# One overflow loop nested by four, one ring slot kept for the next stage's weights, and routing constants loaded once, in a fused two-block transformer kernel

## What is computed

```python
def _hier_moe(t, wr_g, br_g, wr_e, br_e, w_gate, w_up, w_down):
    lg = (t @ wr_g) + br_g                      # 4 groups
    g = argmax(lg); gate_g = softmax(lg)[g]
    le_g = ((t @ wr_e) + br_e).reshape(n_tok, 4, 8)[g]
    top_v, top_i = lax.top_k(le_g, 2)           # 2 of 8 experts in the group
    weights = gate_g * softmax(top_v)
    ...
    hidden = silu(x_blk @ w_gate[e]) * (x_blk @ w_up[e])     # 1024 -> 512
    y = hidden @ w_down[e]                                   # 512 -> 1024
    out[token] += y * weight
```

## Time and profile before

| what | value |
|---|---|
| time, median of 3 runs | 3021.82 us (3021.67 to 3022.43) |
| the profiled execution's own time | 3016.29 us |
| its span in the profile | 3014.4 us |
| PE busy | 2466.3 us, 82% |
| VectorE busy | 999.0 us, 33% |
| ScalarE busy | 560.1 us, 19% |
| GpSimd busy | 175.7 us, 6% |
| data moved by DMA | 591.83 MB, mean 196 GB/s |

### The profile page before, as it was taken

The page is one execution under the profiler, slowest core; times in us unless marked ns, Lnnn a source line. Parts: engine busy times, 40 slices in busy tenths (PEclk is TensorE's granted clock), DMA queues, the critical chain, the costliest instruction groups (busy, mean ns, idle before and its releaser), DMA issues. The chain is left out here.

```text
span 3014.4 us, 30863 instructions
## 1 busy us (share of the span) xinstructions
PE 2466.3 (82%) x11973; PEld 1302.9 (43%) x11973; DVE 999.0 (33%) x2199; ACT 560.1 (19%) x1254; POOL 175.7 (6%) x278
## 2 busy tenths in 40 slices
PE   7999898876977777598985977776696778999999
PEld 2443366444533333245643634333243544444444
DVE  3211276644222222466544222221365343001000
ACT  2000177210000000116510000000123441000000
POOL 0000000001211111000001211111001000000000
PEclk9999999887999999798987999999797789999999
DMA  7554100517999998410238999996500120321210
GB/s 299 179 185 166 60 1 1 212 74 307 415 415 416 416 415 326 178 42 19 72 130 347 414 416 415 415 415 283 211 14 3 46 70 24 143 84 56 84 56 28
DMA packets 143249, 591.83 MB, mean 196 GB/s; under 512 B 21460, under 2 KB 24028, under 8 KB 104192
## 3 DMA queue, kind: packets, MB, share of 16 engines
q1 hardware_dynamic: 132544, 568.83, 48.0%
q0 software_dynamic: 10560, 21.01, 1.9%
HBM read 579.19 MB, written 24.22 MB: 200 GB/s over the span
## 5 line engine op out<-in xcount | busy, mean ns | idle before, releaser
L1776 PE MATMUL moe_down<-moe_wd,moe_hid_t 128*64 128x512 f32 x1024 | 244.0, 620 | 73.2 <-DMA moe_wd<-in_moe_w_down 61.2
L1750 PE MATMUL moe_up<-moe_wu,moe_xg_t 128*64 128x256 f32 x2048 | 236.4, 383 | 62.3 <-DMA moe_wu<-in_moe_w_up 62.1
L1750 PE MATMUL moe_gate<-moe_wg,moe_xg_t 128*64 128x256 f32 x2048 | 240.0, 388 | 53.8 <-DMA moe_wg<-in_moe_w_gate 52.2
L395 PE MATMUL qkv_acc<-qkv_w,a_buffer 128*128 128x512 f32 x576 | 256.2, 598 | 1.4 <-DVE a_buffer L470 1.2
L2637 PE MATMUL mlp_acc<-m_h,mlp_w 128*128 128x512 f32 x512 | 223.1, 596 | 10.9 <-DMA mlp_w<-in_w_up 8.9
L1750 PEld LDWEIGHTS moe_gate<-moe_wg,moe_xg_t 128*64 128x64 f32 x2048 | 154.3, 139 | 161.4 <-DMA moe_wg<-in_moe_w_gate 89.7
L2652 PE MATMUL mlp_acc<-mlp_w,mlp_u_t 128*128 128x512 f32 x512 | 220.0, 592 | 1.4 <-DVE mlp_u_t L2672 1.4
L1750 PEld LDWEIGHTS moe_up<-moe_wu,moe_xg_t 128*64 128x64 f32 x2048 | 151.5, 137 | 143.7 <-DMA moe_wu<-in_moe_w_up 83.2
L395 PEld LDWEIGHTS qkv_acc<-qkv_w,a_buffer 128*128 128x128 f32 x576 | 107.4, 191 | 132.7 <-issue 123.9
L1776 PEld LDWEIGHTS moe_down<-moe_wd,moe_hid_t 128*64 128x64 f32 x1024 | 74.2, 141 | 201.8 <-issue 129.7
L1836 DVE COPY moe_y<-moe_down 128x512 f32<-128x512 f32 x64 | 44.2, 691 | 351.6 <-PE moe_down L1776 351.6
(11 more groups left out here) (360 smaller groups left out, 2838.4 us busy)
## 6 DMA issues: line engine op xcount, KB each, us to landing
moe_wg<-in_moe_w_gate SPq DMA_DIRECT2D x64, 2048.0 KB, 30.5
moe_wu<-in_moe_w_up SPq DMA_DIRECT2D x64, 2048.0 KB, 29.5
moe_wd<-in_moe_w_down SPq DMA_DIRECT2D x64, 2048.0 KB, 30.4
qkv_mod_w<-in_mod_w SPq DMA_DIRECT2D x48, 1024.0 KB, 4.9
mlp_w<-in_w_up SPq DMA_DIRECT2D x8, 2048.0 KB, 9.2
mlp_w<-in_w_down SPq DMA_DIRECT2D x8, 2048.0 KB, 7.8
qkv_w<-in_a_w_qkv SPq DMA_DIRECT2D x12, 1024.0 KB, 9.3
in_w<-in_w_in SPq DMA_DIRECT2D x4, 2048.0 KB, 19.0
```

The costliest lines, as they stand in the source:

```text
L395: mm = nc.tensor.matmul(acc[i % 4][:], h_t[:, k, t * P:(t + 1) * P], w[:, c % w_ring, k, :], start=(k == 0), stop=(k == KD - 1))
L1750: mm = nc.tensor.matmul(acc[b][halves[f], 0:HF], xg_t[b][:, k, c, :], w[:, c, k, f * HF:(f + 1) * HF], start=(c, k) == (0, 0), stop=(c, k) ...
L1776: mm = nc.tensor.matmul(down[b][halves[c], :], hid_t[:, k, h, :], wd[z][:, 2 * h + k, c * NCHUNK:(c + 1) * NCHUNK], start=(k, h) == (0, 0) ...
```

## The change

Three things change.

1. `before`, `iota`, `rowid` and `half` become buffers that live through the program. They are loaded in `qkv0`, right behind `ones`; the four loads and the two waits for them leave `route0` and `route1`.
2. Slot 0 of the ring holds expert 0 and no other expert of that layer. Experts 1 to 31 alternate between slots 1 and 2, so expert i waits for expert i - 2. Behind its last refill SP waits for `downed` >= 1 and loads 3 x 2 MB of the next stage's weights into slot 0: all of `b_w_qkv` in layer 0, three of the five chunks of `w_in_2` in layer 1. `qkv1` and `in2` read these chunks from there; `in2` loads the other two itself.
3. The overflow loops become `while_left`: `nx // 4` turns (6 and 4), the four bodies nested in each other's condition, so that a turn without overflow makes one test.

```diff
-            sp.dma_start(e["ones"][:], e["c_ones"]).then_inc(s["ones_in"], 16)
+            for name in ("ones", "before", "iota", "rowid", "half"):
+                sp.dma_start(e[name], e[f"c_{name}"]).then_inc(s["ones_in"], 16)
...
-            loads = [
-                (before[:], e["c_before"]), (iota[:], e["c_iota"]), (rowid[:], e["c_rowid"]),
-                (half[:], e["c_half"]),
-            ]
-            for dst, src in loads:
-                sp.dma_start(dst, src).then_inc(s["const_in"], 16)
...
-            pe.wait_ge(s["const_in"], 16 * 4)
...
-            dve.wait_ge(s["const_in"], 16 * 4)
...
+def slot_and_fill(i):
+
+    return (0, 1) if i == 0 else (1 + (i + 1) % 2, (i + 1) // 2)
+
+
+def next_chunks(ring):
+
+    flat = [ring["wg"][0][:].rearrange("p c k n -> p (c k n)"),
+            ring["wu"][0][:].rearrange("p c k n -> p (c k n)"),
+            ring["wd"][0][:].rearrange("p k n -> p (k n)")]
+    return [x.rearrange("p (k n) -> p k n", k=KD) for x in flat]
...
+def while_left(eng, nx, n, one):
+
+    with eng.Fori(0, nx // 4) as i4:
+        with eng.If(4 * i4 < n):
+            one(i4, 0)
+            with eng.If(4 * i4 + 1 < n):
+                one(i4, 1)
+                with eng.If(4 * i4 + 2 < n):
+                    one(i4, 2)
+                    with eng.If(4 * i4 + 3 < n):
+                        one(i4, 3)
...
             for i in range(RING, NE):
-                refill(i - RING + 1, i % RING, i)
+                refill(i - 1, slot_and_fill(i)[0], i)
+            sp.wait_ge(s["downed"], 1)
+            view = next_w.rearrange("(k p) n -> p k n", p=P)
+            for c, dst in enumerate(next_chunks(ring)):
+                sp.dma_start(dst, view[:, :, c * NCHUNK:(c + 1) * NCHUNK]).then_inc(
+                    ring["next_in"][c], 16)
...
-            with pool.Fori(0, nx // 2) as i2:
-                for b in range(2):
-                    i = NE + 2 * i2 + b
-                    with pool.If(2 * i2 + b < n):
-                        pool.wait_ge(s["turned_x"], i + 1)
...
+            def one_extra(i4, j):
+                i, b = NE + 4 * i4 + j, j % 2
+                pool.wait_ge(s["turned_x"], i + 1)
...
+            while_left(pool, nx, n, one_extra)
...
-        w = ph.sb("w", [P, 3, KD, NCHUNK])
+        w = next_chunks(ring)
...
-            for c in range(3):
-                sp.dma_start(w[:, c], view[:, :, c * NCHUNK:(c + 1) * NCHUNK]).then_inc(loaded[c], 16)
...
             for c, (n0, width) in enumerate(chunks):
-                sp.dma_start(w[:, :, n0:n0 + width], view[:, :, n0:n0 + width]).then_inc(loaded[c], 16)
+                if c >= 3:
+                    sp.dma_start(w[c], view[:, :, n0:n0 + width]).then_inc(loaded[c], 16)
```

More of the change, by code:

```diff
@@ L1391, in route @@
     with Phase(nc, f"route{layer}") as ph:
[L1392 to L1395, removed]
+        before, iota, rowid, half = (e[x] for x in ("before", "iota", "rowid", "half"))
         gate_t = ph.sb("gate_t", [P, nt, NG])
@@ L1611, in load_down, with experts @@
     sp.dma_start(ring["wd"][b][:], src).then_inc(ring["d_in"][b], 16)
-def experts(nc, e, layer, nt, r, ring):
+def while_left(eng, nx, n, one):
[8 more added lines that the diff above has]
+                        one(i4, 3)
+def experts(nc, e, layer, nt, r, ring, next_w):
     nx = max_extra(nt)
-    extra_slot = [(NE + b) % RING for b in range(2)]
-    extra_fill = [(NE + b) // RING + 1 for b in range(2)]
+    extra = [(NE + b, *slot_and_fill(NE + b)) for b in range(4)]
     HF = FE // 2
@@ L1668, in _, with one_extra @@
             for i in range(RING, NE):
-                refill(i - RING + 1, i % RING, i)
-            n = count_of(sp)
-            with sp.Fori(0, nx // 2) as i2:
-                for b in range(2):
[L1673 to L1676, removed]
+                refill(i - 1, slot_and_fill(i)[0], i)
[4 more added lines that the diff above has]
+                    ring["next_in"][c], 16)
+            n = count_of(sp)
+            def one_extra(i4, b):
+                i, z, _ = extra[b]
+                x = sp.value_load(r["expert"][0:1, bass.ds(4 * i4 + b, 1)], min_val=0,
+                                  max_val=NE - 1)
+                refill(i + 4 * i4 - 1, z, x)
+            while_left(sp, nx, n, one_extra)
         @block.gpsimd
@@ L1813, in _ @@
             n = count_of(act)
-            with act.Fori(0, nx // 2) as i2:
-                for b in range(2):
-                    with act.If(2 * i2 + b < n):
-                        one_block(NE + 2 * i2 + b, b, True)
+            while_left(act, nx, n, lambda i4, j: one_block(NE + 4 * i4 + j, j % 2, True))
         @block.vector
@@ L1840, in _ @@
             n = count_of(dve)
-            with dve.Fori(0, nx // 2) as i2:
-                for b in range(2):
-                    with dve.If(2 * i2 + b < n):
-                        one_block(NE + 2 * i2 + b, b, True)
+            while_left(dve, nx, n, lambda i4, j: one_block(NE + 4 * i4 + j, j % 2, True))
 def mod_part(e, layer, part):
@@ L1918, in enter_layer_1 @@
         s = {x: ph.sem(x) for x in names.split()}
-        loaded = [ph.sem(f"loaded{i}") for i in range(3)]
         block = ph.block()
@@ L2090, in _ @@
                 if i == 0:
-                    pe.wait_ge(loaded[c], 16)
+                    pe.wait_ge(ring["next_in"][c], 16)
                 if j == first[i]:
@@ L2117, in layer_1 @@
                 sb("b_v", [P, NT, 4 * HD], F32) as v:
-            enter_layer_1(nc, e, last_r, h_t, q_t, k_t, v)
+            with last_ring["first"]:
+                enter_layer_1(nc, e, last_r, last_ring, h_t, q_t, k_t, v)
             window_attention(nc, e, q_t, k_t, v, o)
@@ L2128, in layer_1 @@
         route(nc, e, 1, stream, logits, r, ring)
-        experts(nc, e, 1, TX, r, ring)
+        experts(nc, e, 1, TX, r, ring, e["w_in_2"][0])
     logits_scope.close()
-    return r
+    return r, ring
 RUNS2 = [(0, 8), (1184, 8), (1952, 6)]
@@ L2188, in enter_block_2 @@
         s = {x: ph.sem(x) for x in names.split()}
-        loaded = [ph.sem(f"loaded{i}") for i in range(n_chunks)]
+        loaded = ring["next_in"] + [ph.sem(f"loaded{i}") for i in range(3, n_chunks)]
         block = ph.block()
@@ L2678, in _, with block_2 @@
                 nc.vector.tensor_tensor(dst, dst, acc[i][:], ALU.add).then_inc(added, 1)
-def block_2(nc, e, r):
+def block_2(nc, e, r, ring):
     stream = list(range(TC, NT))
@@ L2689, in block_2 @@
                 ExitStack() as stack:
-            enter_block_2(nc, e, r, buffer, hh, mq, mk, mv)
+            with ring["first"]:
+                enter_block_2(nc, e, r, ring, buffer, hh, mq, mk, mv)
             q_t = stack.enter_context(sb("c_q", [P, 10, SEQ], F32))
```

58 lines of the change are left out of this document (29 added, 29 removed).

## The result

The changed kernel took 3028.5 us (median of 20 runs, 3022.74 to 3034.28) against 3022.79 us for the kernel before (20 runs in the same jobs): a ratio of 1.002, 95% interval 1.0013 to 1.0027, so 3.9 to 8.2 us slower. The forecast was 3026.2, in a range of 3020.5 to 3034.0, from a sum of +4.4 us. The profiled execution of the changed kernel took 3027.6 us, span 3025.7, which is 11.3 more than the profile before.

The account below looks back on a forecast made before the run. Expert stages were taken as bound by DMA weight loads at 415 GB/s. 24.6 - 8.1 - 7.7 - 5.4 + 1.0 = +4.4 us on the profiled 3016.3 gave 3020.7, as a median 3026.2 us, range 3020.5 to 3034.0.

Parts of the forecast that it names:

- The ring: Expert stages: without slot 0 the first refill and so the last load come 12.29 us later per layer, +24.6 us.
- rival E: Expert plateau: two slots starve the load queue now and then, +24.8 us (3046), or 3036 if once; chance 0.06.
- rival D: Expert stages' ends: two slots let DMA engines drift apart less, 5.1 us less per layer, 3016.0 us; chance 0.09.
- The constants: Start of both routing stages: VectorE no longer waits for constant loads, 3.4 and 4.7 us saved, -8.1 us.
- The loops: Ends of both expert stages: fewer overflow tests on POOL save 4.6 us in layer 0, 3.1 in layer 1, -7.7.
- lower bound of 2.9: Expert stages' ends: smallest saving from nested overflow tests, 2.2 + 0.7 us, with scatter landings near the median of 6.7.
- upper bound of 9.8: Expert stages' ends: largest saving from nested overflow tests, 5.4 + 4.4 us.
- I take 4.3: Expert stages' ends: assumed landing time in us of the last scatter beside the next stage's weights; shortest seen 2.6.
- a sign of being right: Expert stages' ends: the last scatter landing in 3.5 to 5 us would show the forecast right.
- rival B: Early weights collide with the stage's end: scatter lands at 6.7 us, next start 3 later, in2 gain halved; +13.9; chance 0.11.
- The loads ahead: Early weights: in2's two PE stalls and lower clock go, -5.4 us; next phases' first results queue 0.5 later per layer, +1.0.
- rival C: Overflow loops: PE's jumps across four nested bodies miss instruction fetch repeatedly, +24.1 us (3046); chance 0.04.

Follow-up runs that it names:

- the second pair of profiles: Both kernels, before and changed, run again without any edit for a second profile each: 3022.34 us (ratio 1.0001) and 3031.29 us (ratio 1.0027).

## Why the prediction was right

**The ring, +24.6: right in cause and size.** The first refill came 12.3 us later after the barrier in layer 0 (25.69 for 13.39) and 12.6 in layer 1 (24.62 for 11.98; 12.4 and 12.9 in the second pair of profiles), and giving the slot back took 11.6 and 11.8 us out of the stages. The queue's two slots were enough: nothing starved (rival E), the plateau moves 414 to 417 GB/s. The stream from first refill to last load was even 3.4 us shorter in layer 0. Most of that isn't the ring's: kernels with three slots and constants have 476.1 to 477.1, with two slots 475.4, the kernel before 478.9. So some 1 us goes with the two slots (rival D said 5.1 a layer), and the rest with something that isn't the ring.

**The constants, -8.1: right in the first pair of profiles**, with 3.5 and 4.8 us. The second pair has 3.4 and 3.5, so layer 1's 4.7 is met in one pair and missed by 1.2 in the other. The loads are hidden in the first stage.

**The loops, -7.7: the term that was mis-sized.** It gave 1.8 + 1.4 = 3.1, near the lower bound of 2.9. The loop itself was as computed: without weights ahead the two ends gave 9.6, near the upper bound of 9.8. The step that failed is "I take 4.3" for the landing, a number worked out from no row: the scatter landed 7.0 us after its issue in layer 0 and 6.2 in layer 1, outside the 3.5 to 5 us given as a sign of being right. So the end followed rival B's landing of 6.7, while the rest of B (the start 3 us late, `in2`'s gain halved) didn't come. That the cause is the weights queued ahead was shown: 4.4 and 3.3 us from scatter to drain without them and with one chunk, 6.1 to 7.7 with two and three. Of the two landings at hand, 2.6 and 6.7 us, that with the full queue was the neighbour and not that on idle DMA, since the stretch at 392 GB/s is the plateau going on.

**The loads ahead, -5.4 and +1.0: right in cause, the sizes in part.** `in2` became 5.1 us shorter in the first pair of profiles and 3.4 in the second, in which the kernel before has the two stalls but not the lower clock: the 5.4 is met in the one, and in the other only the stalls are there to gain (3.2 us), as in the forecast's lower value of 3.75. The +1.0 didn't come. The next stage's first results and gates weren't late: VectorE in `qkv1` waited 9.04 us for them, 9.01 before, and PE's first matmuls of `in2` start 23.11 us behind the barrier, 23.15 before.

**The sum.** By stages: -3.5 - 4.8 + 7.1 + 10.5 - 5.1 = +4.2 for the two routing stages, the two expert stages and `in2`, against +3.9 for them ahead (the sum of 4.4 less the 0.5 of `qkv1`). The mis-sized loops (4.6 less gain) and the shorter stream (4.3 more) nearly cancel, so that the total came closer than its terms was luck. The second pair gives -3.4 - 3.5 + 6.8 + 10.7 - 3.4 = +7.2. The medians say +5.7 and, in the last job, +8.2; `out1`'s 2.4 is in them and was in no term.

**The branch (rival C) didn't decide.** PE's long test came once in layer 0's stage (4.712 us) and once in layer 1's (4.600), wasn't repeated in the other turns (0.221), and PE was at its barrier 2.9 us before POOL in layer 0. One long jump and then only short ones is what the rule of the Trainium skill, "Runtime: NRT & Kernel Launch", section "Instruction fetch mechanics", gives for a taken branch whose target isn't fetched yet. The traces agree. Every PE test over 2 us in the 12 profiles, 21 in all, has one packet of 16 KB of the instruction queue in it or begun 0.5 us ahead of it, and ends 1.3 to 1.5 us after that packet; in the kernel with the loops alone it is the only packet that moves during layer 0's test (3.857 us).

## What to carry to other kernels

- In a stage bound by one queue of transfers, ask when the queue first gets work that isn't dependent on computing: a ring slot taken away for good costs the delay of its first refill in full, and the same slot taken away only when the last refills can do without it cost nothing here.
- A load put ahead of a barrier also stands ahead of the small writes for which that barrier waits. Here 2 MB were through in time, and 4 MB were not: a few rows that share one late engine with the weights hold up the whole wait. Where a wait behind such a load is for a small transfer, putting that one first may give the same as all the early weights.
- A sum of terms should be compared with its stages and not only with the total, and with two profiles of each kernel: stages that no edit touches differed by 2 to 4 us.

## What the runs showed of the hardware

- A false test across four nested bodies cost PE 4.712 us once in layer 0's stage and 4.600 once in layer 1's, and 0.221 the other times; before, across one body, the longest was 0.387 in layer 0 and 2.302 in layer 1 (2.987 in the second profile). The long test across four bodies took 3.3 to 3.9 us in the kernels with no or one chunk ahead and 4.5 to 4.7 with two or three: its 16 KB packet started 0.9 to 1.3 us into the test in the former and 1.9 to 2.2 in the latter.
- SP was held up in issuing a 2 MB load for 15.34 us, about three loads of 5.05 us, behind its last refills; in the kernel before the longest issue of an expert's load was 9.58 us.
- POOL's drain ahead of the barrier took 5.45 to 5.46 us in both expert stages of the two kernels, and less than 0.1 us behind every other stage.
- The granted clock rose up to 3 us earlier or later within `qkv1` from kernel to kernel with the same work of PE ahead of it, and it fell once inside `out1` behind a stall of 1.25 us; together that is up to 4.7 us of a profile.
